# Moving the weight splits of a two-block fp32 kernel from GpSimd to ScalarE and VectorE

## The reference, cut to what matters

```python
proj = h @ w_in[l]
y_a = gmlp_branch(zu, zv, ...) @ w_up_a[l]
y_b = hgrn2_branch(zq, zf, zi, zo, ...) @ w_up_b[l]
x = x + (jax.nn.sigmoid(g_a) * y_a + jax.nn.sigmoid(g_b) * y_b) @ w_out[l]
x = x + jnp.square(jax.nn.relu(rmsnorm(x, norm_ffn[l]) @ w_ff1[l])) @ w_ff2[l]
...
def swiglu(h, wg, wu, wd):
    return (jax.nn.silu(h @ wg) * (h @ wu)) @ wd
```

## Time and profile before

| | us |
|---|---|
| median of 3 runs | 3047.17 (3044.95 to 3049.79) |
| span of the profiled execution, first to last instruction | 3042.2 |
| median less span (start and end of an execution around the span) | 5.0 |
| PE busy | 2802.1 (92%) |
| POOL busy | 2290.2 (75%) |
| DVE busy | 1319.3 (43%) |
| ACT busy | 475.0 (16%) |
| mean granted TensorE clock | 0.955 of full speed |

### The profile page before, as it was taken

How to read it: one execution, slowest core, us unless ns; L and a number is a source line. 1 busy time by engine, 2 the same in 40 slices (tenths; PEclk the granted TensorE clock), 3 DMA queues, 4 the chain that set the end, 5 groups by cost and what they waited for, 6 DMA issues and landing times.

```text
span 3042.2 us, 32794 instructions
## 1 busy us (share of the span) xinstructions
PE 2802.1 (92%) x12573; PEld 2285.8 (75%) x12573; DVE 1319.3 (43%) x1089; ACT 475.0 (16%) x615; POOL 2290.2 (75%) x994
## 2 busy tenths in 40 slices
PE   6988989988888869999896899998999989999998
PEld 5877868866676648888683788886888868778887
DVE  7887831277877882111507521115211155431112
ACT  3333321110100131000214210002100020120000
POOL 5644559878898958888764588887888878878886
PEclk8989999999898989999997999999999999999999
DMA  3211122257666723322220133322222222322222
GB/s 113 70 41 55 49 63 97 97 182 247 236 231 241 240 100 97 97 97 90 82 90 21 56 97 97 97 90 77 95 97 97 90 90 97 96 83 97 96 89 78
DMA packets 252087, 323.39 MB, mean 106 GB/s; under 512 B 5622, under 2 KB 242420, under 8 KB 243828
## 3 DMA queue, kind: packets, MB, share of 16 engines
q1 hardware_dynamic: 240740, 245.51, 25.0%
q10 hardware_dynamic: 11280, 76.94, 7.2%
HBM read 320.34 MB, written 2.10 MB: 106 GB/s over the span
## 4 chain that ended last, share of the span: by engine, by line
PE 73%; DVE 14%; issue 5%; POOL 4%; ACT 2%; DMA 1%; ACTq 0%; DVEq 0%; SPq 0%; POOLq 0%
PE po L651 19%; PE po L653 19%; PE po L652 19%; DVE ada_acc L1673 3%; PE po L630 3%; PE po L625 2%; PE po L626 2%; POOL w_lo L563 2%; POOL w_hi L560 2%; DVE nt L1374 1%; PE pm L771 1%; DMA ada_in<-in_w_ada_dram 1%; DVE ql L1537 1%; DVE kl L1541 1%; DVE stats L1355 1%
## 5 line engine op out<-in xcount | busy, mean ns | idle before, releaser
L560 POOL TENSOR_TENSOR w_hi<-w_raw,zero 128x1024 fp32r<-128x1024 f32 x472 | 1047.0, 2218 | 694.7 <-issue 267.5
L563 POOL TENSOR_TENSOR w_lo<-w_raw,w_hi 128x1024 fp32r<-128x1024 f32 x472 | 1227.0, 2600 | 37.0
L651 PE MATMUL po<-a_hi,w_hi 128*128 128x512 f32 x1792 | 702.0, 392 | 10.7 <-ACT ev L1230 5.7
L652 PE MATMUL po<-a_lo,w_hi 128*128 128x512 f32 x1792 | 699.0, 390 | 0.0
L653 PE MATMUL po<-a_hi,w_lo 128*128 128x512 f32 x1792 | 698.8, 390 | 0.0
L651 PE MATMUL po<-b_hi,w_hi 128*128 128x512 f32 x1152 | 464.7, 403 | 68.7 <-DVE b_lo L1708 38.2
L653 PE MATMUL po<-b_hi,w_lo 128*128 128x512 f32 x1152 | 459.2, 399 | 0.0
L652 PE MATMUL po<-b_lo,w_hi 128*128 128x512 f32 x1152 | 457.5, 397 | 0.0
L651 PEld LDWEIGHTS po<-a_hi,w_hi 128*128 128x128 f32 x1792 | 337.3, 188 | 84.9 <-issue 7.6
L653 PEld LDWEIGHTS po<-a_hi,w_lo 128*128 128x128 f32 x1792 | 337.5, 188 | 71.0
L652 PEld LDWEIGHTS po<-a_lo,w_hi 128*128 128x128 f32 x1792 | 337.5, 188 | 70.5 <-issue 0.7
(11 more groups left out here) (251 smaller groups left out, 2812.2 us busy)
## 6 DMA issues: line engine op xcount, KB each, us to landing
ada_in<-in_w_ada_dram ACTq DMA_DIRECT2D x64, 1152.0 KB, 5.3
w_raw<-in_ffn_wg_dram SPq DMA_DIRECT2D x44, 1024.0 KB, 5.3
w_raw<-in_ffn_wu_dram SPq DMA_DIRECT2D x44, 1024.0 KB, 5.3
w_raw<-in_w_ff_dram SPq DMA_DIRECT2D x32, 1024.0 KB, 5.5
w_raw<-in_ffn_wd_dram SPq DMA_DIRECT2D x32, 1024.0 KB, 5.2
w_raw<-in_w_in_dram SPq DMA_DIRECT2D x28, 1024.0 KB, 5.1
w_raw<-in_ffn_wd_dram SPq DMA_DIRECT2D x16, 768.0 KB, 4.7
w_raw<-in_w_in_c_dram SPq DMA_DIRECT2D x12, 1024.0 KB, 5.0
```

Of the source, the lines that this page charges most:

```text
L560: pool.tensor_tensor(w_hi[:, s, part], w_raw[:, s, part], zero8[:, 0:1].to_broadcast([P, UNIT // 2]), ALU.add).then_inc(split_done, 1)
L563: pool.tensor_tensor(w_lo[:, s, part], w_raw[:, s, part], w_hi[:, s, part].bitcast(F32), ALU.subtract).then_inc(split_done, 1)
L651: pe.matmul(o, wh, hi[:, k, :], start=(k == ks[0]), stop=False)
L652: pe.matmul(o, wh, lo[:, k, :], start=False, stop=False)
```

## The change

GpSimd makes no splits any more. `weight_hi(un, halves, s)` on ScalarE rounds the halves with a Copy activation, `weight_lo(un, halves, s)` on VectorE subtracts. The one semaphore `split_done` (4 steps a unit) becomes `hi_done` and `lo_done` (2 steps a unit each): TensorE and the loads of SP wait for `lo_done`, VectorE's subtraction for `hi_done`, ScalarE's rounding for the landing and for unit `un-2` to be finished. Since both engines' queues are in order, each call has a place written out by hand: 2 + 2 operations a unit, 944 in all as before, always in unit order. GpSimd keeps the constants and the pooling windows. Besides, VectorE makes the first norm ahead of the level masks instead of after them, and ScalarE's loop over the four FF groups becomes a loop over three and a last one without the calls that the last norm takes over.

```diff
@@ gpsimd: removed, with its calls splits(2, U_ABO + 2) and splits(U_ABO + 2, U_END)
-            def split(s, landed, free, before):
-                pool.wait_ge(raw_landed[s], landed)
-                if free is not None:
-                    pool.wait_ge(chunk_done, free)
-                for h in range(2):
-                    part = slice(h * UNIT // 2, (h + 1) * UNIT // 2)
-                    pool.tensor_tensor(w_hi[:, s, part], w_raw[:, s, part],
-                                       zero8[:, 0:1].to_broadcast([P, UNIT // 2]), ALU.add).then_inc(split_done, 1)
-                    pool.wait_ge(split_done, before + (2 * h + 1))
-                    pool.tensor_tensor(w_lo[:, s, part], w_raw[:, s, part], w_hi[:, s, part].bitcast(F32),
-                                       ALU.subtract).then_inc(split_done, 1)
@@ sync and tensor
-                    sp.wait_ge(split_done, free * 2)
+                    sp.wait_ge(lo_done, free)
-                pe.wait_ge(split_done, at(un, 4, 2))
+                pe.wait_ge(lo_done, at(un, 2, 1))
@@ scalar
+            def weight_hi(un, halves=(0, 1), s=0):
+                for h in halves:
+                    part = slice(h * UNIT // 2, (h + 1) * UNIT // 2)
+                    if h == 0:
+                        act.wait_ge(raw_landed[s], at(un - s, 8, 16))
+                        if not (isinstance(un, int) and un < 2):
+                            act.wait_ge(chunk_done, at(un, 2, -2))
+                    act.activation(w_hi[:, s, part], w_raw[:, s, part], ACT.Copy).then_inc(hi_done, 1)
@@ scalar, norm: in the squares, and in the a_hi loop
+                    if u0 is not None and k in ((4,) if name == "final" else (0, 2, 4)):
+                        weight_hi(u0 + 2 + k // 2, s=(k // 2) % 2)
...
+                    if k in (2, 4):
+                        if name == "mix":
+                            weight_hi(1, (k // 2 - 1,), s=1)
+                        elif u0 is not None:
+                            weight_hi(u0 + 5, (k // 2 - 1,), s=1)
@@ scalar, HGRN2 pair: behind evac(0), after level 6, behind evac(2), behind evac(3)
+                        weight_hi(p * 4 + (U_HG + 6), s=0)
+                        weight_hi(p * 4 + (U_HG + 7), s=1)
+                weight_hi(p * 4 + (U_HG + 8), s=0)
+                    weight_hi(p * 4 + (U_HG + 9), s=1)
@@ scalar, FF group
                         act.activation(ev[:, k % 2, :], po[:, k % 2, :, :]..., ACT.Relu).then_inc(out_taken[k % 2], 2)
+                        weight_hi(un + 2, (0,), s=k % 2)
                         act.wait_ge(s_f_dve, ff_dve.after(f"hid{k}", g))
                         act.activation(b_hi[...], hid[:, :], ACT.Copy).then_inc(s_f_act, ff_act.one(f"hi{k}"))
+                        weight_hi(un + 2, (1,), s=k % 2)
+                    elif not last or k < 6:
+                        weight_hi(g * 8 + (U_FF + 2 + k), s=k % 2)
                     if k + 2 < DK:
                         load_ada(k + 2)
@@ vector
+            def weight_lo(un, halves=(0, 1), s=0):
+                for h in halves:
+                    part = slice(h * UNIT // 2, (h + 1) * UNIT // 2)
+                    dve.wait_ge(hi_done, at(un, 2, h + 1))
+                    dve.tensor_tensor(w_lo[:, s, part], w_raw[:, s, part], w_hi[:, s, part].bitcast(F32),
+                                      ALU.subtract).then_inc(lo_done, 1)
@@ vector, HGRN2 pair: at levels 1 and 3, after keep(LV - 1), ahead of the wait for rso
+                        weight_lo(p * 4 + (U_HG + 5), s=1)
+                        weight_lo(p * 4 + (U_HG + 6), s=0)
+                weight_lo(p * 4 + (U_HG + 7), s=1)
+                weight_lo(p * 4 + (U_HG + 8), s=0)
@@ vector, FF group: after hid, after b_lo; after the residual of units 4 to 7
+                        weight_lo(un + 2, (0,), s=s)
+                        weight_lo(un + 2, (1,), s=s)
+                        if not last or k < DK - 2:
+                            weight_lo(un + 2, s=s)
                     if k + 1 < DK:
                         add_ada(g, k + 1, last=last)
@@ vector, SwiGLU loop: ahead of the wait for unit un+1, after hid, after b_lo
+                        weight_lo(un + 2, s=0)
+                        weight_lo(un + 3, (0,), s=1)
+                        weight_lo(un + 3, (1,), s=1)
@@ vector, norm: at k = 6 and after the last a_lo
+                    if k == DK - 2 and u0 is not None:
+                        weight_lo(u0 + 5, (0,), s=1)
+                elif u0 is not None:
+                    weight_lo(u0 + 5, (1,), s=1)
@@ vector: in residual, after unit v
+                    if v < 2 or (more and (v == 2 or then is None)):
+                        weight_lo(u0 + v + 2, s=s)
@@ attention: scalar and vector, ahead of the first scores
+                weight_hi(U_ABO + v, s=v)
+            for v in range(4):
+                weight_lo(U_AB + 6 + v, s=v % 2)
```

More of the change, by code:

```diff
@@ L1123, in pair @@
                             evac(1, p + 1)
-                    elif more:
-                        gate_step(p + 1, "lq")
-                        gate_step(p + 1, "rq")
+                    else:
+                        if more:
+                            gate_step(p + 1, "lq")
+                            gate_step(p + 1, "rq")
+                        weight_hi(p * 4 + (U_HG + 7), s=1)
                 act.wait_ge(s_h_dve, hg_dve.after(f"K{LV - 1}", p))
@@ L1212, in _, with hidden_group @@
                     .then_inc(s_m_act, mix_act.one("mh"))
-            norm("ffn")
-            with act.Fori(0, FFG) as g:
+            norm("ffn", U_OUT)
+            def hidden_group(g, last=False):
                 def load_ada(k):
@@ L1234, in _, with ffn @@
                                        ACT.Copy).then_inc(s_f_act, ff_act.one(f"hi{k}"))
+                        weight_hi(un + 2, (1,), s=k % 2)
+                    elif not last or k < 6:
+                        weight_hi(g * 8 + (U_FF + 2 + k), s=k % 2)
                     if k + 2 < DK:
                         load_ada(k + 2)
-            norm("final")
-            def ffn(l, j):
-                norm(f"{l}{2 * j}")
+            with act.Fori(0, FFG - 1) as g:
+                hidden_group(g)
+            hidden_group(FFG - 1, last=True)
+            norm("final", U_FF + 8 * FFG - 4)
+            def ffn(l, j, before):
+                norm(f"{l}{2 * j}", before)
                 for g, n in enumerate(GROUPS):
@@ L1338, in _ @@
                     .then_inc(s_c_act, cv_act.one("hi"))
-            ffn(1, 1)
+                weight_hi(u0 + 4, s=u0 % 2)
+            ffn_out = ffn(1, 1, U_CO)
+            for v in range(2):
+                weight_hi(ffn_out + v + 2, s=v)
         @block.vector
@@ L1386, in norm, with residual @@
                     lo(k - 1)
+                    if k == DK - 2 and u0 is not None:
+                        weight_lo(u0 + 5, (0,), s=1)
                 lo(DK - 1)
-            def residual(u0, gates=None, then=None):
+                if name == "mix":
+                    weight_lo(1, s=1)
+                elif u0 is not None:
+                    weight_lo(u0 + 5, (1,), s=1)
+            def residual(u0, gates=None, then=None, more=True):
                 for v in range(4):
@@ L1434, in halves @@
                 return buf.rearrange("p (b n) -> p b n", n=2 * h)
+            weight_lo(0, s=0)
+            norm("mix")
             dve.wait_ge(consts_ready, 14)
@@ L1761, in ffn @@
                                           ALU.subtract).then_inc(s_w_dve, fd.one("lo"))
-                    last = g == len(GROUPS) - 1 and (l, j) != (1, 1)
+                        weight_lo(un + 3, (1,), s=1)
+                    last = g == len(GROUPS) - 1
                     residual(U_FFN[l, j, g] + n, gate[:, 3 * l + 2 * j, :],
-                             {(0, 0): "01", (0, 1): "10", (1, 0): "11"}[l, j] if last else None)
+                             {(0, 0): "01", (0, 1): "10", (1, 0): "11"}[l, j] if last and (l, j) != (1, 1) else None,
+                             more=not last or (l, j) != (1, 1))
+                return U_FFN[l, j, len(GROUPS) - 1] + GROUPS[-1]
             dve.wait_ge(norm_dve["final"].sem, norm_dve["final"].end)
-            ffn(0, 0)
-            norm("01")
+            ffn_out = ffn(0, 0, None)
+            norm("01", ffn_out)
             for k in range(15):
@@ L1790, in _ @@
                         .then_inc(out_taken[s], 1)
+                weight_lo(U_AB + v + 2, s=s)
+            for v in range(4):
+                weight_lo(U_AB + 6 + v, s=v % 2)
             dve.wait_ge(s_a_act, at_act.after("lam"))
```

86 lines of the change are left out of this document (57 added, 29 removed).

## The result

The changed kernel takes 2879.4 us (median of 4 runs, 2878.7 to 2881.1), the kernel before 3046.1 us beside it: a ratio of 0.946, 95% interval 0.9445 to 0.9475. The medians differ by 167 us; forecast were 137 us and 2910 us. The profiled execution's span is 2876.6 us, 165.6 us less than that of the kernel before.

A forecast was written before the change was run, and what follows sets the result against it. VectorE, slowed by GpSimd's split reads, was taken to leave TensorE idle in the FF stage, HGRN2 pairs and norms. Terms -71 - 24 - 27 - 5 - 3 - 2 - 4 - 3 + 2 = -137 gave 2910 us, range 2862 to 2960.

The forecast's parts named there:

- (b): FF stage, pairs and norms: fewer gaps keep the clock at its upper level, more is won, 2863 us; chance 0.16.
- The mechanism: Whole kernel: GpSimd's SBUF reads block VectorE's two-input operations through a shared port pair; removing the splits gives VectorE's fast speed.
- (d): VectorE's slow speed stays, coming from something else; FF loop 20 us, time above 3150 us; chance 0.02.
- The costs of the added work: 472 Copies on ScalarE at 1.06 us each and 472 subtractions on VectorE at 1.23 us each.
- The FF stage: Four FF groups: a group goes from 115.6 to 97.5 us, hidden loop from 14.96 to 11.8; -71 us.
- The HGRN2 pairs: Four pairs: 6 us each, between 0 and 16, as one gap goes and the others stay; -24 us.
- The norms: From nt to the first unit's end: 16.0 us; -5.8 for three, -3.3 for three others, -27 in all.
- The last norm of block one: Ahead of the first MLP: shorter sums -9, two units' Copies and subtractions in its chain +5; -4 us.
- The start: Kernel's start: six sums of squares each 1.5 us shorter and masks out of the way; -5 us (0 to -9).
- (a): Queue order takes back half: HGRN2 gives 0 instead of -24, norms -15; 2946 us; chance 0.20.
- (c): FF stage's 32 steps: ada_in loads late behind ScalarE's Copies; slower from 4.3 us a step, up to 3080 us; chance 0.05.

The follow-up runs named there:

- relu_first: Changed kernel with the FF stage's load of ada_in for the next step moved behind the next hidden unit's Relu in ScalarE's queue; 2855.4 us, ratio 0.938.
- twice: Changed kernel with every subtraction of the HGRN2 pairs done twice on VectorE; 2906.6 us, ratio 0.955.
- pairs_reads: Changed kernel with eight unneeded GpSimd operations of 128x512 reading SBUF for each of units 2 to 15, HGRN2 stage alone; 2914.7 us, ratio 0.958.
- the fastest kernel: Changed kernel with ada_in loads behind the next Relu and the first MLP's two units out of block one's last norm chain; 2852.2 us, ratio 0.937.

## Why the prediction was right, and where its sizes were off

The measured 2879 us lies in the stated range, 2862 to 2960 us, but outside the narrower 2885 to 2935 us that the prediction gave to its forecast alone. It is about two thirds of the way from the forecast (2910) to rival (b) (2863).

**The mechanism** was right and is shown from both sides: take GpSimd's reads away and VectorE runs at its fast speed; put reads back in one stage and that stage slows down; put writes back and nothing happens. Rival (d) is out. What is not separated is how the 165.6 us divide between VectorE's speed and TensorE's direct waits for the splits (some 20 us). By the pages of the two profiles, 111 us are gaps of TensorE and 55 us shorter matmul time at the higher clock.

**The costs of the added work** (1.06 and 1.23 us) were measured at 1.05 and 1.22.

**The FF stage**, -71 and -3.3 for its norm, gave -81.8. A group takes 94.4 us (forecast 97.5): head 17.2 us (18.9), first to fourth Relu 34.8 (35.4), to the end of `b_lo` 4.7 (4.8), from there to the last residual 37.7 (38.4). The head was off most: the first `ada_acc` pair takes 2.74 us instead of 6.08, and I had taken off 1.8. The loop was right to 2%, but I read its issue and handover (0.64 us; by the times given beside it 0.68) as a fixed part of it; it was ScalarE's queue, and `relu_first` takes it out.

**The HGRN2 pairs** are the step that failed: "I take 6 us a pair, between 0 and 16, since the gap at the earlier trace rows goes and the others stay". The others went too. The four pairs gave 3.9, 16.3, 14.5 and 6.6 us, each from the last `nt` of the one ahead (the first from the first norm), the whole stage 41 for 24. So 6 us was about right for the outer two, and the middle two came near the upper bound of 16.4. I had seen one gap of three, and left the clock out of the sum although I had priced it at 7.4 us. In the third pair before the change, TensorE was busy 73.2 of 82.7 us at a clock of 0.92; after it 68.0 of 68.3 at 1.00. So 9.2 us came from gaps and 5.2 from the clock. An operation that I had not looked at, the eight scans at the head of a pair, went from 10.2 to 2.6 us. What could have been seen: 446 us of waiting inside VectorE's instructions, where I counted on some 250 (VectorE at 1650 us forecast, 1436 measured). The mechanism behind the other gaps is the same: the three before the change (2.6, 1.4 and 5.6 us in that pair) all end with `kl`.

**The norms**: 14.2 to 14.6 us from `nt` to the end of the first unit, as in the one without splits, not 16.0. So the inserted Copies and the subtraction cost nothing that shows. Two of the three long ones gave 7.2 and 6.9 us for 5.8; the third, with attention's first scores behind it, 4.7 for 3.8.

**The last norm of block one**: I set +5 for two units in the chain against -9 for shorter sums. Behind the last residual only two sums were long (3.93 us for the two, 1.47 after); the others took 0.69 us in both the earlier trace rows, so most of the -9 was not there to be won. It lost 2 us.

**The start** gave 9 us for 5: the last sum of squares ends at 20.8 us instead of 28.7, and the rest comes from the level masks, 7 us of VectorE's work that stood ahead of the first `nt`. No run separates the new order from the faster sums.

**The rivals.** (a), that the order of the queues takes half back, did not happen, but `twice` shows that it was less than 2.4 us away at a level. (b) was right in kind for the pairs: the clock went to 1.00, and a pair gave 10.3 us on average where (b) has 12 and the forecast 6. Of its 2 us more for a norm some 1 us came. In the FF groups a gap and a clock of 0.96 to 0.98 stayed, as the forecast had it. That the total came near (b) is in part luck, since the 7.5 us more of the FF stage came from its norm and from the head and the loop of a group, which (b) does not name. (c) did not happen: 4.0 us of waiting in all; made real, at 2.0 us a step, it costs 1 us a step against `relu_first`, so it is far from its 4.3.

## What to carry to other kernels

A wide spread between the durations of equal instructions can be a wait hidden in busy time. Compare the shortest with the mean and sum the difference over the kernel: in the trace before it is 358 us on VectorE, of the 446 that went. What is missing lies in groups where every instruction was slow, above all the 44 `b_lo` of the SwiGLU MLPs (2.74 us each, 1.23 after), so compare groups of the same operation and shape as well. The sum is what the engine can get back, not the kernel, which got 167 us: TensorE waited 0.8 us in all for those `b_lo`. Before pricing a stretch, count all the gaps of one period and the low-clock time behind each, since they go together. After such a change look again at what releases each short operation: moving a load in a queue gave nothing that could be told when VectorE was slow (ratio 0.9989) and 24 us once it was fast.

## What the runs showed of the hardware

**The two engines take turns, an instruction each.** In `pairs_reads` two streams of back-to-back operations alternate strictly, so a short operation suffers most. Beside the old splits a scan of 128x128 goes from 0.40 us to between 2.05 and 2.55, `de` from 0.68 to 2.4, `ada_acc` of 2304 columns from 2.6 to 4.5. GpSimd's side stretches as well: its operation on 512 columns takes 1.04 us alone or beside the scans and 1.37 beside `de`, `ql` and `kl`, and a `w_lo` split took 2.40 us with no VectorE operation beside it and 2.60 on average. 512 columns of memset, which take no turn, take 0.53.

**What is held and what is not.** Held beside GpSimd reads: operations with two tiles in SBUF, the scans, and also the first `ada_acc` operation, which has one tile in SBUF and a column of scalars: 1.41 us alone, 2.89 before the change (groups by line, before and after):
```profile
L1670 DVE TENSOR_SCALAR ada_acc<-ada_in,c_act 128x2304 f32<-128x2304 f32 x8 | 22.9, 2888 | 1.5 <-DMA ada_in<-in_w_ada_dram 1.5
```
```profile
L1729 DVE TENSOR_SCALAR ada_acc<-ada_in,c_act 128x2304 f32<-128x2304 f32 x8 | 11.1, 1413 | 2.1 <-DMA ada_in<-in_w_ada_dram 2.1
```
Two more forms with one tile in SBUF were held: the copy `stats` (1.09 us on average before, 0.42 after) and `cy<-cv,cols` (1.76, 0.49). Not held: transposes (2.57 us before and after), reductions (2.55), `COPY_PREDICATED` (in `pairs_reads` 0.88 us on average beside GpSimd and 0.89 without it), and operations with one tile in PSUM and one in SBUF (`hid<-ev,po`, 1.22 and 1.22). The Trainium skill (SBUF — State Buffer, "Who interferes with whom") says that `tensor_scalar` can enter a mode with two ports and then contends, that `tensor_reduce` on this chip never does, and that a GpSimd instruction which only writes does not contend with VectorE's two-input ones; the rows agree with all three (1.41 against 2.89, 2.55 against 2.55, 2879.1 against 2879.3 us).

**The busier the DMA engines, the later `ada_in` landed, and little of it was waited for.** It lands in 5.3 us before the change (236 GB/s in an FF group), 5.7 after it (290), and 6.5 in the fastest kernel (308); VectorE waits 10 us for it there in all.
